# A hybrid decoder trunk: the transposes of tiles 0 to 3 between the matmuls ahead of each channel mixer issued one token tile later

## What is computed

```
for i in range(2):
    h = rms_norm(x, norm_mix_pre[i])
    m = chunked_gmlp(h, ...) @ w_out   if i == 0 else   stick_breaking_attention(h, ...) @ w_out
    x = x + rms_norm(m, norm_mix_post[i])          # post-norm, then the residual sum
    h = rms_norm(x, norm_ffn_pre[i])               # pre-norm
    f = square(relu(h @ mlp_w1[i])) @ mlp_w2[i]    # 1024 -> 4096 -> 1024
    x = x + rms_norm(f, norm_ffn_post[i])
```

## Time and profile before

| | |
|---|---|
| median of three runs | 2761.81 us |
| profiled execution | 2760.58 us, of which span 2758.8 us |
| TensorE (PE) busy | 2549.0 us, 92% of the span |
| VectorE (DVE) | 1535.4 us, 56% |
| POOL | 1116.4 us, 40% |
| ScalarE (ACT) | 1029.6 us, 37% |
| first boundary with a channel mixer's start | about 600 to 687 us |
| second | about 2047 to 2123 us |

### The profile page before, as it was taken

The page is one execution under the profiler, slowest core; times in us unless marked ns, Lnnn a source line. Parts: engine busy times, 40 slices in busy tenths (PEclk is TensorE's granted clock), DMA queues, the critical chain, the costliest instruction groups (busy, mean ns, idle before and its releaser), DMA issues.

```text
span 2758.8 us, 35462 instructions
## 1 busy us (share of the span) xinstructions
PE 2549.0 (92%) x13100; PEld 2155.2 (78%) x13100; DVE 1535.4 (56%) x1959; ACT 1029.6 (37%) x1507; POOL 1116.4 (40%) x716
## 2 busy tenths in 40 slices
PE   7999999897999989999899968888997999989997
PEld 7997777776888868887898856667796888868886
DVE  3215666659655567777411134555338655577775
ACT  4223112125444433334212146767425444333332
POOL 2221221225555555555222143444235555465554
PEclk9999999999999999999999989999999999999999
DMA  5222112122444464353223624444113444464443
GB/s 161 92 91 92 62 46 77 61 84 96 164 149 149 140 226 165 131 188 121 98 92 148 202 87 112 100 100 97 54 54 100 167 150 156 145 234 142 150 161 122
DMA packets 180417, 342.56 MB, mean 124 GB/s; under 512 B 12224, under 2 KB 95168, under 8 KB 178240
## 3 DMA queue, kind: packets, MB, share of 16 engines
q1 hardware_dynamic: 173632, 311.47, 34.8%
q10 hardware_dynamic: 6656, 29.36, 2.6%
HBM read 235.95 MB, written 104.86 MB: 124 GB/s over the span
## 4 chain that ended last, share of the span: by engine, by line
PE 77%; DVE 9%; issue 5%; ACT 4%; POOL 2%; DMA 2%; SPq 0%; DVEq 0%; ACTq 0%; POOLq 0%
PE psum L1113 21%; PE psum L1156 20%; PE psum L931 13%; PE psum L918 9%; PE psum L942 5%; PE psum L1244 3%; DVE stick L2066 2%; PE psum L1214 2%; PE psum L1231 2%; DVE vst L1808 2%; ACT psum L1611 1%; PE psum L1035 1%; ACT brk L1605 1%; POOL rw_lo L875 1%; DVE acc L1688 1%
## 5 line engine op out<-in xcount | busy, mean ns | idle before, releaser
L1156 PE MATMUL psum<-rw_hi,ra_hi 128*128 128x512 f32 x896 | 353.4, 394 | 17.9 <-POOL rw_lo L875 9.4
L788 POOL TENSOR_TENSOR w_lo<-stage,w_hi 128x1024 fp32r<-128x1024 f32 x56 | 137.3, 2473 | 531.2 <-ACT w_hi L1301 531.2
L1156 PE MATMUL psum<-rw_lo,ra_hi 128*128 128x512 f32 x896 | 351.9, 393 | 0.0
L1156 PE MATMUL psum<-rw_hi,ra_lo 128*128 128x512 f32 x896 | 351.6, 392 | 0.0
L875 POOL TENSOR_TENSOR rw_lo<-blk,rw_hi 128x512 fp32r<-128x512 f32 x160 | 238.9, 1524 | 196.9 <-ACT rw_hi L1442 196.9
L2066 DVE TENSOR_TENSOR_SCAN stick<-psum,brk 128x128 f32<-128x128 f32 (+7 forms) x128 | 173.4, 1356 | 172.6 <-ACT psum L1611 171.1
L891 POOL TENSOR_TENSOR brk<-brk,stick 128x128 f32<-128x128 f32 (+7 forms) x128 | 153.4, 1207 | 234.1 <-DVE stick L2066 220.5
L1437 ACT ACTIVATE ra_hi<-a_raw 128x2048 fp32r<-128x2048 f32 x56 | 107.3, 1917 | 358.0 <-PE psum L1156 266.8
L1953 DVE TENSOR_TENSOR ra_lo<-a_raw,ra_hi 128x512 fp32r<-128x512 f32 x224 | 229.0, 1031 | 19.8 <-ACT ra_hi L1437 19.8
L931 PE MATMUL psum<-w_hi,hT_hi 128*128 128x256 f32 x768 | 220.1, 287 | 1.4 <-DVE hT_lo L2073 1.4
L931 PE MATMUL psum<-w_lo,hT_hi 128*128 128x256 f32 x768 | 218.9, 285 | 0.0
(11 more groups left out here) (225 smaller groups left out, 6453.3 us busy)
## 6 DMA issues: line engine op xcount, KB each, us to landing
a_raw<-a_forms SPq DMA_DIRECT2D x56, 1024.0 KB, 6.5
a_forms<-a_out SPq DMA_DIRECT2D x64, 512.0 KB, 3.1
blk<-mlp_w_in SPq DMA_DIRECT2D x32, 1024.0 KB, 5.4
a_forms<-a_out SPq DMA_DIRECT2D x32, 768.0 KB, 3.3
stage<-a_w_in_in SPq DMA_DIRECT2D x16, 1024.0 KB, 5.4
stage<-mlp_w_in SPq DMA_DIRECT2D x16, 1024.0 KB, 6.0
raw<-mlp_w_in SPq DMA_DIRECT2D x32, 512.0 KB, 5.8
x_res<-xt SPq DMA_DIRECT2D x24, 512.0 KB, 4.9
```

The costliest lines, as they stand in the source:

```text
L788: pool.tensor_tensor(w[b][1][:, c], raw[:, c], w[b][0][:, c].bitcast(F32), ALU.subtract).then_inc(unit_ready, 1)
L1156: mm = pe.matmul(psum[:, down_bank(n, tp), :], ring_a[n % 3][sa][:, k, tp * P:(tp + 1) * P], ring_w[n % 3][sw][:, k, :], start=(p in (1, 2 ...
```

## The change

Everything that handles the transposed tiles 0 to 3 of a boundary (TensorE, ScalarE, VectorE) moves from the steps 3 to 6 to the steps 4 to 7. Behind the gMLP the fourth group of transposes stands behind the last matmuls, as the loop on TensorE ends at tile 6.

```
 # TensorE, behind the gMLP
-                if t >= 3:
-                    quad(1, 0, 1, t - 3)
-                    quad(1, 0, 2, t - 3)
+                if t >= 4:
+                    quad(1, 0, 1, t - 4)
+                    quad(1, 0, 2, t - 4)
             first_chunk(2 * NT - 2)
             first_chunk(2 * NT - 1).then_inc(tail_first, 1)
             second_chunk(2 * NT - 2)
             second_chunk(2 * NT - 1)
+            quad(1, 0, 1, HALF_T - 1)
+            quad(1, 0, 2, HALF_T - 1)
 # TensorE, behind attention
-                    if last and 3 <= t <= 6:
-                        if t == 3:
+                    if last and t >= 4:
+                        if t == 4:
                             pe.wait_ge(dve_evac, FI_END - NT - FI_V2)
-                        quad(3, 1, 1, t - 3)
-                        quad(3, 1, 2, t - 3)
+                        quad(3, 1, 1, t - 4)
+                        quad(3, 1, 2, t - 4)
 # ScalarE, both boundaries (between square_m(b, t) and square_x(b, t - 1))
-                    if 3 <= t <= 6:
-                        quad_take(layer, 1, t - 3)
-                        quad_take(layer, 2, t - 3)
+                    if t >= 4:
+                        quad_take(layer, 1, t - 4)
+                        quad_take(layer, 2, t - 4)
 # VectorE, both boundaries (behind post_norm(b, t))
-                    if 3 <= t <= 6:
-                        quad_split(layer, 1, t - 3)
-                        quad_split(layer, 2, t - 3)
+                    if t >= 4:
+                        quad_split(layer, 1, t - 4)
+                        quad_split(layer, 2, t - 4)
```

## The result

The changed kernel ran 2778.69 us in the median of four runs (2774.28 to 2779.93), against 2761.93 for the kernel before in its four: a ratio of 1.0057, 95% interval 1.0045 to 1.0070, that is 12 to 19 us slower. A second series of five runs gave 2777.01 against 2762.81, ratio 1.0042 (1.0028 to 1.0056). The profiled execution of the changed kernel took 2774.28 us, span 2772.5, 13.7 more than before.

What follows compares the result with a forecast made beforehand. TensorE was taken to bound the kernel (77% of the chain). Terms of 4.95 and 7.7 us summed to 12.65, carried whole to the end: 2774.5 us in the median, chance 0.80, range 2768 to 2780.5.

Steps and rivals of the forecast that it cites:

- The gate must now wait for post_norm(7) and a pair of splits: Start of each channel mixer's first product on TensorE; claimed 4.95 us later behind the gMLP, 7.7 us later behind attention.
- the 1.55 us: First boundary: how much earlier VectorE was to finish post_norm(7), with POOL's weight part moving up equally.
- The other side: Rival: TensorE's stalls in both boundaries were on the path, so 7.7 us come off, 2754.1 us; chance 0.03.
- the absorption behind the gate: Rival: VectorE leads behind the first product, so only its own lateness counts, +0.85 us, 2762.7 us; chance 0.05.
- The term of the first boundary: Behind the gMLP, the channel mixer's first product starts 4.95 us later; bounds +3.9 and +7.35.
- The 0.45 us of step 3: First boundary, VectorE: gain from step 3 losing its pair of splits, 0.45 us instead of 1.20 because of POOL's addition.
- The 1.10 us from the waits for tiles 5 and 6: First boundary: VectorE's waits for TensorE of 0.28 and 0.82 us fall away, a gain of 1.10 us.
- my upper bound of 7.35: First boundary: first product 7.35 us later if TensorE resumes tile 6 at the low clock for 5.25 us.
- The term of the second boundary: Behind attention, the channel mixer's first product starts 7.7 us later; bounds +6.5 and +8.7.
- the addition's hold: A VectorE multiplication started under POOL's addition is held until 1.08 us behind its end, so step 3 gains nothing behind attention.
- The late tile 6 that I put at up to 1 us net: Second boundary: at the low clock TensorE's tile 6 is 1.4 us late, of which about 1 is passed on.
- The clock at the products, taken as 0: Products behind both first-product starts: clock effect could be -2.4 to +2.4 and -1.8 to +3.1 us; taken as 0.

Runs made afterwards that it cites:

- one-boundary kernels: Two kernels: the change made only behind the gMLP, or only behind attention, against the kernel before; ratios 1.0016 and 1.0028 (+4.4 and +7.7 us).
- gMLP boundary only: The change made only behind the gMLP, with attention's boundary as in the kernel before; ratio 1.0016 (1.0004 to 1.0028), +4.4 us.
- Four banks: The changed kernel, with the first eight transposed pieces behind the gMLP on four PSUM banks instead of two; ratio to the kernel before 1.0049.
- stop alone removed: Kernel before, behind the gMLP only: four PSUM banks, transposes of tiles 0 and 1 one step later, tiles 2 and 3 both in step 6; ratio 0.9997.
- only last pair late: The kernel before, with only VectorE's two splits of tile 3 moved from step 6 to step 7, behind post_norm(7); ratio 1.0043, +12 us.

## Why the prediction was right, and where it was off

**The direction and the mechanism held.** "The gate must now wait for post_norm(7) and a pair of splits": shown by the releaser and by the place of the two splits, and by the kernel in which those two alone were moved. The stop of 3.49 us was off the path, as the kernel without it shows: its gate is 1.6 to 1.7 us earlier, which is the 1.55 us by which VectorE and POOL were to move up, and not 3.5. The other side (the stall was on the path) and the absorption behind the gate are both refuted: what was lost at the first gate, 6.74 us, was 6.72 at the boundary's end, and the one-boundary kernels add up to nearly the whole.

**The term of the first boundary was too small: 4.95 forecast, 6.74 measured.** The step that failed is the gain of 1.55 us that VectorE was to have. The 0.45 us of step 3 came: the first copy of tile 4 stands 16.04 us behind the copies of tile 2 (635.38 - 619.34), where it stood 16.47 before (635.35 - 618.88).

```profile
635.35 0.68 DVE L1802 TENSOR_TENSOR acc<-psum,acc 128x512 f32<-128x512 f32 x1
```

The 1.10 us from the waits for tiles 5 and 6 did not stay, and took the 0.45 along: the forecast had tile 6 done at 640.9 "against 642.5 before", but TensorE resumed at the low clock, was done at 642.95, and the copy at 643.14 waited 1.66 us; it stands 23.80 us behind the copies of tile 2, before 23.77. The low stretch lasted about 3.3 us (the matmuls start 0.42 us apart up to 638.03, then 0.23), less than the 5.25 of my upper bound of 7.35. I took the high clock for the main line because the gap of 3.49 us at 622.52 had not lowered it. Here a gap of 2.87 did, one of 2.12 (gMLP boundary only) did not: 56.34 against 57.42 at the gate, for the same list. Four banks take the gap away, and there the term comes out: from the copies of tile 2 the gate is 39.12 - 34.27 = 4.85 us later than before. So the forecast of VectorE's list was right to 0.1 us, and what the sum lacked is the returned wait with the low clock behind it, 1.8 us. Most of that is the clock: in the gMLP-only kernel TensorE resumed equally late, 15.7 us behind the copies of tile 2, but at the high clock, and its gate is at 39.53, 1.4 us ahead of the changed kernel's 40.90. The low clock was in the bounds and not in the sum.

**The term of the second boundary was right: 7.7 forecast, 7.85 measured at the gate.** That step 3 gains nothing there was read from the addition's hold: the multiplication at 2076.02 now takes 3.07 us instead of 1.91 and ends no earlier. The late tile 6 that I put at up to 1 us net cost VectorE a wait of 0.57, and net nothing: post_norm(7) was over 40.98 us behind the landmark, before 40.97. The next multiplication, at 2087.69, started later by that, but now near the end of the POOL addition that had held it, and took 1.28 us instead of 1.91, which the forecast had not seen. By the rule of the Trainium skill, "SBUF — State Buffer", section "SBUF: two separate sides", the held instruction starts when the other ends; the multiplications at 630.61 and 2076.02 end 1.09 us behind POOL's additions, where 1.28 is the length without a hold, so these traces agree with it to 0.2 us, as before.

**The clock at the products, taken as 0:** 8.06 us before and 8.06 after for the two products behind the first gate (660.24 to 668.30), 7.44 and 6.93 behind the second. So an idle time of 8.35 us cost no more than one of 4.18. That step held in this trace, with some luck: the second trace of the changed kernel has 8.10 and 7.37, the other kernels 7.0 to 8.5 and 7.0 to 8.4. The 0.5 us is the difference between 7.85 and 7.36.

**The sum: 12.65 forecast, 13.7 in the trace, 16.8 in the first series, 11.6 and 14.2 in the second by ratio and median.** That the sum is 1.1 us from the trace owes something to the second term, whose low clock cost nothing net. The measured 2778.69 lies 4.2 us above the forecast of 2774.5, inside the range, near its end. Of this 1.1 us is the trace. The rest is a difference between executions of one kernel: the profiled one was the shortest of its series, at a mean clock of 0.972; the runs of 2779.4 and 2779.93 had 0.970. At half speed a stretch shows 0.5, so 0.002 less in the mean is 0.004 of the span at the low clock instead of the high one, of which half is lost: 5.5 us, about what they differ by (an estimate, as the clock is given to three places).

## What to carry to other kernels

A stall is worth what waits behind it. Before removing one, look at the next wait of the same engine: if another engine ends that one, the time only moves there. When work is moved one step later to fill a stall, follow the last item of the group through every queue it is in, for it is that item that passes behind the dearest work, and the gate that needs it moves by all of that. And an instruction freed early may still be held to the same end, as VectorE's multiplications were by POOL's additions.

## What the runs showed of the hardware

The spread between executions has a place. In all traces of the table the other stages that I measured repeat within 1 us (302.8 to 303.6 us for the up phase of the first channel mixer, 296.7 to 297.0 for its down phase, 75.53 to 75.55 for the output projection), but attention takes from 374.9 to 381.7 us with the same instructions. Windows of attention in the kernel with the stop alone removed and in the one with four banks (start:end, us, busy us of the engines, granted clock, share of the DMA engines, GB/s):

```profile
1836.00:1883.00 47.00, 39.73 (x231) 31.76 (x231) 26.81 (x23) 32.85 (x63) 21.10 (x18) 1.00 0.45 108
1883.00:1930.00 47.00, 41.53 (x244) 33.28 (x243) 25.80 (x22) 33.78 (x64) 19.83 (x17) 1.00 0.42 99
```

```profile
1845.00:1892.00 47.00, 39.70 (x219) 31.44 (x218) 26.15 (x22) 32.34 (x61) 19.30 (x18) 0.96 0.41 101
1892.00:1939.00 47.00, 41.51 (x227) 33.26 (x226) 24.81 (x22) 31.56 (x58) 21.00 (x18) 0.94 0.43 101
```

The whole stage has the same work (1730 and 1728 matmuls recorded), but these two windows hold 475 matmuls in the first kernel and 446 in the second, at a clock of 1.00 and of 0.96 and 0.94. Short low stretches come or not in a stage in which TensorE waits 44.6 to 44.8 us for VectorE in 53 small stops. Four windows in a row of the second kernel are below 1.00, by 0.04, 0.04, 0.06 and 0.01; of 47 us each that is 7.1 us lost (an estimate), about the 6.7 by which its attention is longer. Those 6.7 us are part of the 23.6 between these two profiled spans. They are half as much as the effect under study, in a stage that no kernel here changes. With differences of 0.2 to 0.5% the distance between two landmarks inside a stage told more than the total.

After a gap TensorE's clock was not to be told from the gap's length: 3.49 us left it high (3.51 and 3.46 in two other traces), 2.87 lowered it (2.86 and 2.90 in two others), 2.12 did not; after 8.35 us idle the first product behind the gate took 5.3 us, after 4.18 it had taken 5.25, and after 9.55 and 12.75 us (only last pair late, four banks) 4.3 and 4.2. In those last two the product (1, 1) then took 4.4 us instead of 2.9, so the low clock came later rather than not at all.
